# Fourteen conditioning vectors summed by VectorE from 256 KB pieces, in feed-forward and odd mixer

## The reference, cut to what matters

```python
c_act = jax.nn.silu(c)                                  # 1024 numbers
for layer in range(DEPTH):                              # 2
    mod = c_act @ cond_w[layer] + cond_b[layer]         # (1024) @ (1024, 6144)
    sh_m, sc_m, g_m, sh_f, sc_f, g_f = [m[:, None, :] for m in jnp.split(mod, 6, axis=-1)]
    h = x * (1.0 + sc_m) + sh_m
    y = even_mixer(h, ...) if layer % 2 == 0 else retention_mixer(h, ...)
    x = layer_norm(ALPHA * x + g_m * y, ln_w[layer, 0], ln_b[layer, 0])
    h = x * (1.0 + sc_f) + sh_f
    y = swiglu(h, ...) if layer % 2 == 0 else moe_swiglu(h, ...)
    x = layer_norm(ALPHA * x + g_f * y, ln_w[layer, 1], ln_b[layer, 1])
```

## Time and profile before

| | us |
|---|---|
| runs, median of 3 (lowest to highest) | 1742.06 (1741.53 to 1742.91) |
| profiled execution: its time, its span | 1742.85, 1740.9 |
| TensorE busy | 1617.3 (93%) |
| VectorE busy | 1282.3 (74%) |
| ScalarE busy | 1009.3 (58%) |
| mean granted clock of TensorE | 0.966 |
| chain that ended last | TensorE 86%, VectorE 7% |

### The profile page before, as it was taken

How to read it: one execution, slowest core, us unless ns; L and a number is a source line. 1 busy time by engine, 2 the same in 40 slices (tenths; PEclk the granted TensorE clock), 3 DMA queues, 4 the chain that set the end, 5 groups by cost and what they waited for, 6 DMA issues and landing times.

```text
span 1740.9 us, 20082 instructions
## 1 busy us (share of the span) xinstructions
PE 1617.3 (93%) x7810; PEld 1297.4 (75%) x7810; DVE 1282.3 (74%) x1160; ACT 1009.3 (58%) x867; POOL 132.8 (8%) x94
## 2 busy tenths in 40 slices
PE   4888996999969999879999999999999999999996
PEld 1874765787858777658888888888888888888875
DVE  1374536655456665688889888898898898988986
ACT  1432223444434444347777777777777777777775
POOL 0421310000000100220000000000000000000005
PEclk8898998999989999979999999999999999999998
DMA  9347885855454543539999999999999999999993
GB/s 329 130 167 283 322 316 193 285 183 185 169 169 146 164 171 145 187 129 391 388 379 390 375 388 387 369 388 379 376 389 375 381 388 371 384 385 367 385 382 151
DMA packets 234370, 515.33 MB, mean 296 GB/s; under 512 B 8936, under 2 KB 40960, under 8 KB 234176
## 3 DMA queue, kind: packets, MB, share of 16 engines
q1 hardware_dynamic: 228272, 491.99, 77.3%
q10 hardware_dynamic: 2992, 11.79, 1.9%
q0 software_dynamic: 3008, 10.20, 1.9%
HBM read 507.15 MB, written 13.11 MB: 299 GB/s over the span
## 4 chain that ended last, share of the span: by engine, by line
PE 86%; DVE 7%; issue 2%; ACT 2%; DMA 2%; POOL 1%; DVEq 0%; SPq 0%; ACTq 0%; POOLq 0%
PE bank L762 25%; PE bank L764 25%; PE bank L763 25%; PE bank L741 2%; PE bank L925 2%; DMA ring<-in_cond_w 2%; PE bank L1185 1%; PE bank L757 1%; DVE arena L1768 1%; DVE small L1689 1%; PE bank L774 0%; ACT w_part L1310 0%; DVE w_part L1643 0%; DVE hs L1715 0%; PE bank L1167 0%
## 5 line engine op out<-in xcount | busy, mean ns | idle before, releaser
L1654 DVE TENSOR_TENSOR w_lo<-ring,w_hi 128x2048 fp32r<-128x2048 f32 x336 | 764.7, 2290 | 104.1 <-ACT w_hi L1537 102.2
L1537 ACT ACTIVATE w_hi<-ring 128x2048 fp32r<-128x2048 f32 x334 | 640.5, 1918 | 196.3 <-PE bank L764 187.0
L762 PE MATMUL bank<-w_lo,heT_hi 128*128 128x512 f32 x896 | 353.8, 395 | 3.8 <-DVE w_lo L1654 2.2
L764 PE MATMUL bank<-w_hi,heT_hi 128*128 128x512 f32 x896 | 349.7, 390 | 0.0
L763 PE MATMUL bank<-w_hi,heT_lo 128*128 128x512 f32 x896 | 348.9, 389 | 0.0
L1643 DVE TENSOR_TENSOR w_part<-ring,w_part 128x1024 fp32r<-128x1024 f32 x148 | 183.4, 1246 | 211.0 <-ACT w_part L1310 206.2
L1310 ACT ACTIVATE w_part<-ring 128x1024 fp32r<-128x1024 f32 (+1 forms) x162 | 169.1, 1049 | 252.0 <-PE bank L764 247.3
L762 PEld LDWEIGHTS bank<-w_lo,heT_hi 128*128 128x128 f32 x896 | 168.3, 188 | 39.0 <-issue 5.9
L764 PEld LDWEIGHTS bank<-w_hi,heT_hi 128*128 128x128 f32 x896 | 168.2, 188 | 35.9
L763 PEld LDWEIGHTS bank<-w_hi,heT_lo 128*128 128x128 f32 x896 | 168.5, 188 | 33.6
L762 PE MATMUL bank<-w_part,hT_hi 128*128 128x512 f32 (+1 forms) x448 | 179.8, 401 | 14.2 <-DVE w_part L1643 13.1
(11 more groups left out here) (344 smaller groups left out, 1586.8 us busy)
## 6 DMA issues: line engine op xcount, KB each, us to landing
ring<-in_moe_w_up SPq DMA_DIRECT2D x224, 1024.0 KB, 8.8
ring<-in_moe_w_down SPq DMA_DIRECT2D x112, 1024.0 KB, 7.8
ring<-in_cond_w SPq DMA_DIRECT2D x24, 2048.0 KB, 9.1
ring<-in_ffn_w_up SPq DMA_DIRECT2D x22, 1024.0 KB, 8.2
ring<-in_od_w_in SPq DMA_DIRECT2D x8, 2048.0 KB, 7.9
ring<-in_ev_w_in SPq DMA_DIRECT2D x5, 2048.0 KB, 12.4
ring<-in_ffn_w_down SPq DMA_DIRECT2D x5, 2048.0 KB, 7.7
ring<-in_od_w_in SPq DMA_DIRECT2D x8, 1024.0 KB, 8.0
```

The source lines that it names most:

```text
L762: mm(bank, lhs[0], rhs[1], start=start, stop=False)
L764: return mm(bank, lhs[0], rhs[0], start=False, stop=stop)
L1537: f(w_hi[:, n % 3], half_landed(act, it, u, half), ACT.Copy) \
L1654: tt(w_lo[:, buf], at, w_hi[:, buf].bitcast(F32), ALU.subtract).then_inc(S["w_lo"], 1)
```

## The change

The fourteen vectors from (0, 10) on leave the ring, bank 7 and the even mixer. Their weights come in 112 pieces of 128x512 (256 KB) into five buffers of their own, `chunks`, and VectorE multiplies each piece by its column of `c` and adds it to `acc` (L1699 of the changed kernel), after a start from the bias (L1695). That leaves 128 partial sums for each column, one in each partition; `cond` adds them and takes them to all partitions with one product with ones. The sums of a unit's four pieces stand behind the splits of the units from feed-forward up 1 to the gate of the fourth head; the broadcasts move to later places, two of them into the router. On GpSimd a bias tile is cleared and loaded. `c` is kept a second time (`cT`). The eight banks rotate from an earlier point. At the end, the first tile's weight and bias go from GpSimd to VectorE. The compiler's scratch for DMA is set to 4096.

```diff
-COND_BATCHES = (tuple((0, u) for u in FIRST_COND), tuple((0, u) for u in range(4, N_COND)),
-                tuple((1, u) for u in range(N_COND)))
+COND_BATCHES = (tuple((0, u) for u in FIRST_COND), tuple((0, u) for u in range(4, 10)))
+SUM_COND = ((0, 10), (0, 11)) + tuple((1, u) for u in range(N_COND))
...
+SPREAD_AT = {
+    ("ffn_up", 3): (0,), ("ffn_up", 5): (1,), ("ffn_up", 7): (2,), ("ffn_up", 9): (3,),
+    ("ffn_down", 1): (4,), ("ffn_down", 3): (5,), ("ffn_down", 5): (6,),
+    ("od_qk", 0): (7,), ("od_g", 0): (8,), ("od_v", 1): (9,), ("od_qk", 2): (10,), ("od_g", 2): (11,),
+    ("router",): (12, 13),
+}
+CHUNKS = 5
...
+        SUM_START = stream_place["ffn_up", 1]
...
             for key in stream_units():
                 s, _ = units[key]
                 if before[key]:
                     slot_read(sp, before[key])
+                while fetched < KC * len(SUM_COND) and fetched < 4 * (stream_place[key] - 2 - SUM_START) + CHUNKS \
+                        and stream_place[key] >= 2 + SUM_START:
+                    (l, u), k, i = SUM_COND[fetched // KC], fetched % KC, fetched % CHUNKS
+                    if fetched >= CHUNKS:
+                        sp.wait_ge(S["chunk_used"], fetched - CHUNKS + 1)
+                    sp.dma_start(chunks[:, i], cond_w[l, P * k:P * k + P, 512 * u:512 * u + 512]).then_inc(chunk_in[i], 16)
+                    fetched += 1
                 load(s, source(key))
...
                 bank, full = to_fill(pe, "cond", l, u)
+                if (l, u) in SUM_COND:
+                    n = SUM_COND.index((l, u))
+                    pe.wait_ge(S["chunk_used"], KC * n + KC)
+                    mm(bank[:], ones, acc[:, n % 2], start=True, stop=True).then_inc(full, 1)
+                    return
...
-            cond_rows(len(cond_order) - rows_next[0])
+            assert rows_next[0] == len(cond_order)
             turn(1, lambda half, t: taken(pe, "pv", t) if half else pe.wait_ge(S["mix_ready"], t + 1), (2, 3, 0, 1))
...
             turned(1, (2, 3, 0, 1))
-            cond_kept(2)
...
                     tt(part_buffer(key, 1), slot_part(dve, key), part_buffer(key, 0).bitcast(F32),
                        ALU.subtract).then_inc(S["w_lo"], 1)
+                    sum_cond(key)
...
+            def sum_cond(key):
+
+                w = stream_place[key[:-1]] - SUM_START
+                if not 0 <= w < KC * len(SUM_COND) // 4:
+                    return
+                for _ in range(2 if key[:-1] == ("ffn_down", 5) else (1, 0, 1, 2)[key[-1]]):
+                    n, k = sums[0] // KC, sums[0] % KC
+                    l, u = SUM_COND[n]
+                    total = acc[:, n % 2]
+                    if k == 0:
+                        filled(dve, "cond", *(SUM_COND[n - 2] if n > 1 else (0, 9)))
+                        dve.wait_ge(S["sum_bias_in"], 16)
+                        col = N_COND * l + u
+                        V.then(ts(total, sum_bias[:], ident[:, col:col + 1], None, ALU.mult))
+                    else:
+                        dve.wait_ge(S["chunk_used"], sums[0])
+                    dve.wait_ge(chunk_in[sums[0] % CHUNKS], 16 * (sums[0] // CHUNKS) + 16)
+                    stt(total, chunks[:, sums[0] % CHUNKS], cT[:, k:k + 1], total, ALU.mult, ALU.add) \
+                        .then_inc(S["chunk_used"], 1)
+                    sums[0] += 1
...
+            affine(3, 0)
             affine(3, 1)
...
+            nc.gpsimd.memset(sum_bias[:], 0.0).then_inc(S["bias_zero"], 1)
+            pool.wait_ge(S["bias_zero"], 1)
+            pool.dma_start(sum_bias[0:2 * N_COND], cond_b.rearrange("l (u n) -> (l u) n", n=512)).then_inc(S["sum_bias_in"], 16)
...
-            pool.wait_ge(S["ln_in"], 32 * 4)
-            pool.wait_ge(S["normed"], 3 * NT + 1)
-            G.then(tt(xs[:, 0], xs[:, 0], ln[:, 0], ALU.mult))
-            tt(xs[:, 0], xs[:, 0], ln[:, 1], ALU.add).then_inc(S["first_done"], 1)
...
-    nc = bacc.Bacc("TRN2", target_bir_lowering=False, num_devices=1)
+    nc = bacc.Bacc("TRN2", target_bir_lowering=False, num_devices=1, dynamic_dma_scratch_size=4096)
```

More of the change, by code:

```diff
@@ L139, in stream_units @@
     e = lambda *n: [("ev_in", i) for i in n]
-    order = c(0, *FIRST_COND) + e(0, 1, 2, 5, 4, 3) + c(0, *range(4, N_COND)) + c(1, *range(N_COND))
+    order = c(0, *FIRST_COND) + e(0, 1, 2, 5, 4, 3) + c(0, *range(4, 10))
     order += [("ev_out", 0), ("ev_out", 1)]
@@ L183, in pe_order @@
         o += ([("ws", n)] if n else []) + ([("kv", n)] if n < 3 else [])
-    o += [("go", t) for t in range(NT)] + [("cond_rows", 2)]
+    o += [("go", t) for t in range(NT)]
     o += [("hT", 1, i) for i in (2, 3, 0, 1)]
@@ L188, in pe_order @@
     for u in range(FFN // 256):
[L189 removed]
+        o += [("ffn_up", u, t) for t in range(NT)] + [("cond", *k) for k in spread_at("ffn_up", u)]
         o += [("ffn_T", u - 1)] if u else []
     o += [("ffn_down", t, h) for t in range(NT) for h in range(2)] + [("ffn_T", FFN // 256 - 1)]
[L192 removed]
+    o += [("cond", *k) for i in range(6) for k in spread_at("ffn_down", i)]
     o += [("hT", 3, i) for i in BY_TILE]
     for h in range(RH):
[L195 removed]
+        o += [("od_qk", h, t) for t in range(NT)] + [("cond", *k) for k in spread_at("od_qk", h)]
         if h:
[L197 removed]
             o += [("ret_y", h - 1, t) for t in range(NT)]
[L199 to L200 removed]
+        o += [("od_v", h, t) for t in range(NT)] + [("cond", *k) for k in spread_at("od_v", h)]
+        o += [("ret_T", h, t) for t in range(NT)]
+        o += [("od_g", h, t) for t in range(NT)] + [("cond", *k) for k in spread_at("od_g", h)] + [("ret_s", h)]
         if h:
@@ L205, in pe_order @@
     o += [("hT", 4, i) for i in BY_TILE]
-    o += [("routerT",), ("router",), ("rank",)]
+    o += [("routerT",), ("router",)] + [("cond", *k) for k in spread_at("router")] + [("rank",)]
     o += [("rows_T", 0), ("rows_T", 1)]
@@ L290, in trunk @@
         half_in = [[ctx.enter_context(nc.semaphore(f"half{h}_in{i}")) for h in range(2)] for i in range(RING)]
+        chunk_in = [ctx.enter_context(nc.semaphore(f"chunk_in{i}")) for i in range(CHUNKS)]
         bank_full = [ctx.enter_context(nc.semaphore(f"bank_full{i}")) for i in range(8)]
@@ L299, in trunk @@
         acc = sb("acc", [P, 2, 512])
+        sum_bias = sb("sum_bias", [P, 512])
+        chunks = sb("chunks", [P, CHUNKS, 512])
         ln = sb("ln", [P, 2, D])
@@ L463, in trunk @@
         assert cond_order == [k for batch in COND_BATCHES for k in batch]
+        stream_place = {k: i for i, k in enumerate(stream_units())}
+        SUM_START = stream_place["ffn_up", 1]
         partial = [k for k in stream_units() if k[0] in ("ffn_down", "od_out") and (k[0], k[1] + 1) in units]
@@ L715, in _ @@
             for t in range(NT):
-                sp.wait_ge(S["ln_done" if t else "first_done"], 3 * NT + 1 if t else 1)
+                sp.wait_ge(S["ln_done"], 3 * NT + t + 1)
                 sp.dma_start(out[0, t * P:(t + 1) * P, :], xs[:, t]).then_inc(S["out_done"], 16)
@@ L758, in cond, with spread @@
                     .then_inc(full, 1)
+            def spread(*key):
+                for l, u in spread_at(*key):
+                    cond(l, u)
             def three(bank, lhs, rhs, start, stop):
@@ L1082, in ffn_between @@
                     ffn_turn(FFN // 256 - 1)
-                if i > 1 and i - 2 in DOWN_COND:
-                    cond(*DOWN_COND[i - 2])
+                spread("ffn_down", i)
                 taken(pe, "ffn_T", min(2 * i + 1, FFN // 256 - 1))
@@ L1149, in _ @@
             narrow("router", logit_rows)
+            spread("router")
             pe.wait_ge(S["late_in"], 16)
@@ L1592, in _ @@
             bank, free = filled(dve, "cT")
+            V.do(nc.vector.tensor_copy(cT, bank[:, 0:KC]))
             nc.vector.tensor_copy(zc[:, :, 31], bank[:, 0:KC]).then_inc(free, 1)
@@ L1648, in split_ahead @@
                 split_to(parts_ahead(key))
+            sums = [0]
+            def sum_cond(key):
[17 more added lines that the diff above has]
+                    sums[0] += 1
             def rest(it, n, slot, buf):
@@ L2043, in _ @@
                     turned_rows(RH - 1)
+            assert sums[0] == KC * len(SUM_COND)
             narrow_lo(rw, 2)
```

40 lines of the change are left out of this document (13 added, 27 removed).

## The result

The changed kernel takes 1750.97 us (median of 5 runs, 1747.49 to 1752.69); the kernel before took 1741.53 beside it (1740.70 to 1742.91). The ratio is 1.0047 [1.0036, 1.0057]: 0.47% or about 8 us slower, where 1738.0 and faster was forecast. The profiled execution is the slowest of the five, 1752.69 us with a span of 1750.8, so its differences to the span of 1740.9 run about 1.7 over those of the medians.

What follows compares the result with a forecast made beforehand. TensorE was taken to set the pace, with row sums on the even mixer's chain. Terms -18.8 + 2 + 2.5 + 10.1 + 2.5 - 1.8 - 0.6 = -4.1 gave a median of 1738.0 us, range 1726 to 1748.

Steps and rivals of the forecast that it cites:

- The eight row sums: Even mixer, 186.56 to 235.67: eight row sums on TensorE's chain go, each giving back 1.85 us, 14.8 in all.
- The others: Even mixer's remaining six row sums: 2.07 us at 178.65, then 1.05, 0.6 and 0.3 at the state; 0 at 172.85.
- the first chunk's stall: Start of feed-forward: chunk 0 shares DMA engines with ScalarE's copies of x, so VectorE's sum and TensorE's next part wait.
- The end: Tail: GpSimd's two operations on the first tile go to VectorE, -0.6 us, range -0.9 to +1.
- Rival D: Slower: chunks hold VectorE in every unit, 1746.4 us at 0.3 lost per unit, 1752 at 0.5; chance 0.2.
- I take +2: Even mixer before the output projection: without row sums TensorE's clock falls, costing 2 us, range 0 to +7.
- rival C: Opened gaps hold the clock low through state updates and output projection's start, +5 on the forecast, 1743 us; chance 0.15.
- 10.1 and 2.5: At the first chunk: TensorE stalls 10.1 us, then loses 2.5 to a lower clock; together 0 to +17.
- the 128th passes at about 332.8: Chunk 0's 128 rows get turns at q1's present packet pace, so its last row passes at about 332.8 us.
- The broadcasts: TensorE: two of fourteen broadcasts move into the router's wait, -1.8 us, range 0 to -1.9; the other twelve stay visible.
- VectorE's sums: Feed-forward and odd mixer: 112 sums of 0.64 us, mostly hidden, cost +2.5 us in all, range 0 to +6.
- The page's rule that I weighed: An engine drains about 9 to 17 descriptors per queue turn, so the first chunk's stall would all but vanish.

Runs made afterwards that it cites:

- copies 4k rows: Changed kernel with ScalarE's six copies of x left in place but in rows of 4 KB, not 32 KB; 1744.63 us, ratio 1.0009 to the kernel before.
- short idle matmuls: `copies in the quiet` plus idle matmuls of 0.43 to 0.85 us in TensorE's gaps of the even mixer; 1727.82 us, ratio 0.9914 to the kernel before.
- copies in the quiet: Changed kernel with the first five chunk loads and six copies of x issued by SP at about 180 us; 1733.77 us, ratio 0.9952 to the kernel before.
- first five early: Changed kernel with the first five chunk loads issued ahead of the output projection's weights, at about 180 us; 1739.36 us, ratio 0.9980 to the kernel before.
- sums eight columns: `copies in the quiet` with each of VectorE's 112 sums working on 8 of its 512 columns; 1728.76 us, ratio 0.9931 to the kernel before.
- filled gaps: Changed kernel with idle 32x512 matmuls, longer than intended, in TensorE's gaps of the even mixer; 1755.80 us, ratio 1.0079 to the kernel before.
- before idle in boundaries: The kernel before, unchanged but for idle matmuls in TensorE's waits at the three boundaries; 1740.02 us, ratio 0.9982 to the kernel before.

## Why the prediction was wrong

**Right.** The eight row sums: 14.7 measured, 14.8 forecast. The others as well, where the clock is full: 2.3 in the first stretch (22.76 before, 20.48 in `copies 4k rows`) for 2.1, and 2.0 in the state's stretch (32.25 before, 30.23 in `short idle matmuls`) for 1.95. The place and mechanism of the first chunk's stall, and that it would be the largest term. The end, -0.7 against -0.6. Rival D's waits in every unit did not come: VectorE waited for one chunk only.

**Wrong, in order of size (in the profiled span, 14.0 us of miss).**
- *The clock in the even mixer*, "I take +2". In the profiled execution it cost about 8.4: 5.1 in the state's stretch, which came out 3.1 longer where 1.95 shorter was due without the clock, 1.0 behind it, and 2.3 in the first stretch, where products ran at half speed (1.71 and 2.71 us where before 0.87 and 1.98). The step "I take +2" failed because I priced two stretches by rows and took the smaller price. The 5.1 are shown: they stand in each trace with this code, and `short idle matmuls` gives back all of them (35.34 to 30.23), and the 1.0 as well. The 2.3 are in part chance, since other executions with the same code there have none of them. The end of my range, +7, which is what rival C had with 0.15, covers the 6.1 without them and not the 8.4.
- *The first chunk*, "10.1 and 2.5". It cost 13.1 of waiting and with the clock 15.5 (227.17 us of feed-forward against 211.65 in `copies in the quiet`). The step that failed is "the 128th passes at about 332.8": the pace of the packets was right to 0.5 us, but the landing came 2.5 us behind that packet, and I had put nothing for this (2.3 us in `copies 4k rows`). Whether the slowest engine makes these 2.5 us stays open. `first five early` gives 9.6 of the 15.5 back (217.62 us of feed-forward) and `copies in the quiet` all.
- *The broadcasts*, "-1.8". Nothing came of it. Twelve stood visible before as now: by my reading the two of the kernel before in the heads had lain in TensorE's wait for VectorE already. Five moved from feed-forward to the odd mixer, which makes most of the 8.0 there. After the move to the router its stretch grew by 0.4.
- *VectorE's sums*, "+2.5". They cost at least 3.7 by `sums eight columns`, at 0.785 us each and not 0.64.
- *What is left*, 1.7 us, is 0.9 in feed-forward and odd mixer together, 0.4 in the router and 0.4 in the experts. The clock of 600 to 650 is 0.97, where it was 1.00 before; the cause of this rest stays open.

With the measured sizes the sum is -18.8 + 8.4 + 15.5 + 3.7 + 0 - 0.7 = +8.1, beside the 9.9 of the span.

The page's rule that I weighed, of turns between queue rows by packets of many descriptors (the Trainium skill, "DMA: Bandwidth & Descriptors", "Queues, rings and completion order"), would have had the chunk through at once. The runs do not show that: 16.9 us beside rows of 32 KB, 10.9 beside rows of 4 KB. By the page's figure a packet of a dozen rows of 32 KB on the other queue would be a long turn of its own (an estimate), so the waits do not refute the rule either; my reading of it counted only the chunk's own packet. The counts side by side, 26 beside 28 and 271 beside 268, are nearer to one for one, and by that alone the 10.9 us are not explained either.

## What to carry to other kernels

Work that is taken off an engine's path gives back its time less what the clock takes in the gaps that open; look at each gap, and fill it with something short if it is free. Filling that outlasts the gap costs more than the clock does: at one boundary here it made the turn 5.5 us late, where the clock is worth about 1. A buffer with one unit of lead is safe from its own queue and still starved by any bulk copy that runs beside it: list all transfers of the time in which it is wanted, and put the bulk ones where the DMA share is near zero. And when you count a queue's packets to find when a transfer is there, add what lies between its last packet and its landing, 2.3 and 2.5 us here. And before a stretch of one trace is put down to a change, compare it between executions of the same code: one took 20.5 to 23.1 us here.

## What the runs showed of the hardware

- Six DRAM-to-DRAM copies whose outer dimension is 2 ran at 51 GB/s and a DMA share of 0.13, what two of sixteen engines have, where the same copies in contiguous form went with 315 GB/s (300 to 310 of the changed kernel); the engine that issued them was held for 99 us.
- Four matmuls of 512 with 32 columns of weights in the same columns of the array took 3.62 us (`filled gaps`); eight in four different groups of columns took 1.85 (L741 before).
- The sum of 128x512 on VectorE took 0.785 us on the mean against 0.64 for the same kind in the boundary; two in a row show as 1.53.
- Idle matmuls in TensorE's waits kept the granted clock at 1.00 through waits of 10.8 and 12.95 us of the kernel before (`before idle in boundaries`, 290 to 310 and 500 to 530), which otherwise ended at 0.50.
